# Last down matrices in three column parts, the final norm's vector applied by feature, other matrices loaded early, the expert list made at another place

## The reference: two decoder layers with experts

```
for i in range(DEPTH):                                   # DEPTH = 2
    mod = silu(c) @ ada_w[i] + ada_b[i]
    sh1, sc1, g1, sh2, sc2, g2 = split(mod, 6)
    h = modulate(x, norm_mix_g[i], sh1, sc1)
    m, S = retention_mixer(...) if i == 0 else gla_mixer(...)
    x = x + g1 * m
    h = modulate(x, norm_ffn_g[i], sh2, sc2)
    f = moe_ffn(h, ...)          # router, 64 experts, top 8, shared expert
    x = x + g2 * f
return rmsnorm(x, final_norm_g), new states
# rmsnorm(x, g) = x * rsqrt(mean(x * x) + 1e-6) * g
# an expert: (silu(x @ w_gate) * (x @ w_up)) @ w_down
```

## Time and profile before

| | |
|---|---|
| median of 3 runs | 1586.08 us (1584.92 to 1588.89) |
| the profiled execution | 1585.7 us, its span 1583.9 us |
| granted TensorE clock, mean | 0.989 of full |
| layer 0, experts | about 356 to 889 us |
| layer 1, experts | about 1030 to 1575 us |
| DMA | 580 MB, 366 GB/s over the span |

### The profile page before, as it was taken

The page is one execution under the profiler, slowest core; times in us unless marked ns, Lnnn a source line. Parts: engine busy times, 40 slices in busy tenths (PEclk is TensorE's granted clock), DMA queues, the critical chain, the costliest instruction groups (busy, mean ns, idle before and its releaser), DMA issues. The chain is left out here.

```text
span 1583.9 us, 29421 instructions
## 1 busy us (share of the span) xinstructions
PE 1492.9 (94%) x11132; PEld 983.6 (62%) x11132; DVE 701.7 (44%) x1998; ACT 357.8 (23%) x760; POOL 92.0 (6%) x117
## 2 busy tenths in 40 slices
PE   6999998999999999999996899999999999999976
PEld 4778765687665566566553587777566566565533
DVE  3204534315465535534354335453754544543543
ACT  3012443203212111111120255431111211211111
POOL 0000100001000000010000000001000000010000
PEclk9999999999999999999998999999999999999998
DMA  9997699429999999999999983999999999999996
GB/s 364 389 370 267 251 399 399 177 106 359 382 418 420 421 420 420 420 419 419 415 389 415 355 285 109 352 361 338 415 418 421 420 420 420 421 418 415 392 411 245
DMA packets 153295, 580.27 MB, mean 366 GB/s; under 512 B 16893, under 2 KB 62113, under 8 KB 104938
## 3 DMA queue, kind: packets, MB, share of 16 engines
q1 hardware_dynamic: 137642, 535.74, 85.5%
q0 software_dynamic: 14912, 40.91, 6.7%
q10 hardware_dynamic: 640, 2.26, 0.4%
HBM read 566.12 MB, written 26.90 MB: 374 GB/s over the span
## 5 line engine op out<-in xcount | busy, mean ns | idle before, releaser
L2544 PE MATMUL ps<-ring,scratch 128*64 128x256 f32 x3008 | 330.6, 380 | 1.3 <-DMA ring<-in_moe_w_up 1.2
L2544 PEld LDWEIGHTS ps<-ring,scratch 128*64 128x64 f32 x3008 | 215.5, 137 | 106.6 <-issue 3.0
L2603 PE MATMUL ps<-ring,scratch 128*64 128x512 f32 x816 | 186.8, 598 | 1.2 <-DVE scratch L2961 0.9
L716 PE MATMUL ps<-hT,ring 128*128 128x264 f32 x768 | 182.1, 392 | 1.3 <-ACT hT L401 1.3
L2501 PE MATMUL ps<-scratch 128*128 128x264 bf16 x1344 | 165.8, 276 | 3.7 <-DVE xT L2864 2.0
L716 PEld LDWEIGHTS ps<-hT,ring 128*128 128x128 f32 x768 | 146.8, 193 | 31.6 <-issue 2.8
L2889 DVE SCALAR_TENSOR_TENSOR scratch<-scratch,ps 128x256 f32<-128x256 f32 x60 | 28.8, 480 | 300.3 <-ACT scratch L2998 279.7
L2501 PEld LDWEIGHTS ps<-scratch 128*128 128x128 bf16 x1344 | 116.7, 97 | 53.7 <-issue 15.4
L2856 DVE TENSOR_TENSOR scratch<-scratch,ps 128x264 f32<-128x264 f32 x224 | 95.3, 428 | 65.0 <-PE ps L2501 64.9
L2603 PEld LDWEIGHTS ps<-ring,scratch 128*64 128x64 f32 x816 | 53.3, 136 | 107.0 <-issue 75.1
L2998 ACT ACTIVATE scratch<-ps 128x256 f32<-128x256 f32 x60 | 23.1, 384 | 390.9 <-PE ps L2544 319.6
(11 more groups left out here) (411 smaller groups left out, 1538.5 us busy)
## 6 DMA issues: line engine op xcount, KB each, us to landing
ring<-in_moe_w_up SPq DMA_DIRECT2D x128, 1024.0 KB, 19.0
ring<-in_moe_w_gate SPq DMA_DIRECT2D x124, 1024.0 KB, 18.1
ring<-in_moe_w_down SPq DMA_DIRECT2D x118, 1024.0 KB, 15.5
ring<-in_ada_w SPq DMA_DIRECT2D x48, 1024.0 KB, 12.5
ring<-in_ret_w_in SPq DMA_DIRECT2D x24, 1024.0 KB, 16.8
ring<-in_state_ret SPq DMA_DIRECT2D x16, 1024.0 KB, 14.6
out_ret_sample<-ring POOLq DMA_DIRECT2D x16, 1024.0 KB, 9.0
ring<-in_gla_w_in SPq DMA_DIRECT2D x12, 1024.0 KB, 11.9
```

The costliest lines, as they stand in the source:

```text
L716: mm = nc.tensor.matmul(k.ps[:, bank, 0:T], w[:, c, m * P:(m + 1) * P], k.h[:, c, :], start=(c == 0), stop=(c == DC - 1))
L2544: mm = nc.tensor.matmul(k.ps[lo:lo + CAP, 2 + p, j * DE:(j + 1) * DE], xg[:, p, c, lo:lo + CAP], w[:, c, :], start=(c == 0), stop=(c == DC ...
L2603: mm = nc.tensor.matmul(k.ps[lo:lo + CAP, 6 + half, :], hid_t[:, p, m, lo:lo + CAP], w[:, m, half * 512:(half + 1) * 512], start=(m == 0), ...
```

## The change

Seven edits, in both expert layers where nothing else is said.

1. The early loads are matrices 2 and 3 of round 0 (the up matrices of experts 0 and 1) in place of 0 and 1; SP issues the two of round 1 that take their ring slots before the third down matrix of round 0, no longer behind it. `AHEAD` is the first down matrix.
2. The product that orders the ranks stands behind one chunk of the second shared up product, no longer behind three; `list_order` comes directly behind the sum of the weights.
3. DVE splits the weights (`w_parts`) behind the shared hidden products; PE's `slots_first` stands behind four chunks of the shared down product, no longer two.
4. In the last round the down matrices come in columns 0 to 511, 512 to 767 and 768 to 1023, each with its own semaphore. PE makes the second part behind chunks 0 and 1, the third behind 2 and 3.
5. ACT squares chunks 0 and 1 between the copies of the parts, the others behind the load of the square root's table.
6. Layer 1: DVE multiplies each chunk of `k.x` by the gain vector, one number a feature, before it is transposed; ACT squares the chunk as it is; PE sums the squares with the squares as weights and one column of ones. The load of the spread gain vector goes.
7. At the end DVE scales three of the four half rows, ACT the fourth and the samples; POOL has no part, and the order of SP's stores is another.

```diff
-EARLY = 2
+EARLY = (2, 3)
-    AHEAD = ("moe_w_down", 2)
+    AHEAD = ("moe_w_down", 0)
+    EARLY_LOADS = [ROUND[i] for i in EARLY]
+    gained = acc
+    final_sq = row_area[:, D:3 * D].rearrange("p (c t) -> p c t", c=DC)
...
+    LAST_PARTS = [(0, 512, 6, 0), (512, 768, 7, 0), (768, 1024, 7, 256)]
...
-        load_until(k, sp, n_sh + 3 + RING - 1)
+        load_until(k, sp, n_sh + 3 + RING - 2)
         sp.wait_ge(s_count, 1)
-        for name, e in ROUND[0:EARLY]:
+        for name, e in EARLY_LOADS:
...
+        load_until(k, sp, n_sh + 3 + RING - 1)
         wait_used(k, sp, n_sh + 1)
...
-        for half in range(2):
-            cols = slice(half * 512, (half + 1) * 512)
+        for i, (c0, c1, _, _) in enumerate(LAST_PARTS):
+            cols = slice(c0, c1)
...
+    def last_down(i):
+        c0, c1, bank, at = LAST_PARTS[i]
+        for m in range(FC):
+            for e, lo in LIGHT_BLOCKS:
+                n = place("moe_w_down", e, LIGHT_PLACE)
+                mm = nc.tensor.matmul(k.ps[lo:lo + 32, bank, at:at + c1 - c0], hid_t[:, 0, m, lo:lo + 32],
+                                      slot(k, n, D)[:, m, c0:c1], start=(m == 0), stop=(m == FC - 1))
...
     def last_spread(pe, follow):
...
+        chunk(0)
+        chunk(1)
+        pe.wait_ge(s_third_quarter, 16 * EPI)
+        last_down(1)
+        chunk(2)
+        chunk(3)
+        wait_light(pe, LAST, "moe_w_down")
+        pe.wait_ge(s_part, 2 * d + 2)
+        last_down(2)
+        for c in range(4, DC):
+            if c == 6:
+                pe.wait_ge(s_part, 2 * d + 3)
+            if follow and c == 4:
+                follow(pe, 0)
+                follow(pe, 1)
+            chunk(c)
+            if follow:
+                follow(pe, c - 2)
...
+    def squares_sum(t, c):
+        t0, n = TOKENS[t]
+        nc.tensor.matmul(k.ps[:, 6 + t, 0:1], final_sq[:, c, t0:t0 + n], ones[:, 0:1], start=(c == 0),
+                         stop=(c == DC - 1))
     def x_rows(pe, c):
+        pe.wait_ge(s_gained, c + 1)
+        for t, (t0, n) in enumerate(TOKENS[0:2]):
+            nc.tensor.transpose(k.ps[:, 2 + 2 * t + c // 4, (c % 4) * P:(c % 4 + 1) * P], gained[:, c, t0:t0 + n], ident)
+        pe.wait_ge(s_squares, c + 1)
+        squares_sum(0, c)
+        for b in range(DC // 2 + 1) if c == DC // 2 else range(c, c + 1) if c > DC // 2 else ():
+            squares_sum(1, b)
...
-        shared(1, 1, range(LIST_AT))
+        shared(1, 1, range(1))
         pe.wait_ge(s_ranked, 1)
...
+            if beside and i < BESIDE_COPIES:
+                act.wait_ge(s_add, DC * (LAST + 1) + i + 1)
+                beside(act, i)
...
+        def gain(c):
+            nc.vector.tensor_scalar(gained[:, c, :], k.x[:, c, :], k.fin_g[:, c:c + 1], None, ALU.mult)\
+                .then_inc(s_gained, 1)
...
         if layer:
+            for c in range(DC):
+                nc.tensor.transpose(k.ps[0:NS, c // 4, (c % 4) * P:(c % 4 + 1) * P], gained[:, c, TP:T], ident)
+            pe.wait_ge(s_squares, DC + 1)
+            for c in range(DC):
+                mm = nc.tensor.matmul(k.ps[0:NS, 6, 1:2], small[:, c, :], ones[:, 0:1], start=(c == 0),
+                                      stop=(c == DC - 1))
```

More of the change, by code:

```diff
@@ L317, in load_early @@
 def load_early(k, sp, layer):
-    for i in range(EARLY):
-        n = k.stage[f"moe{layer}"] + i
+    for i, at in enumerate(EARLY):
+        n = k.stage[f"moe{layer}"] + at
         wait_slot(k, sp, n - RING)
@@ L1943, in gla, with rows, store @@
     release_semaphores(k, old)
[L1948 to L1968, removed]
 def final(k, behind):
     nc, out = k.nc, k.out
-    s_ms, s_rt, s_rs, s_half, s_scaled, s_small, s_st = (k.sem(f"y_{n}") for n in (
-        "meansq", "root", "rstd", "half_rows", "samples_scaled", "samples", "stored"))
+    s_ms, s_rt, s_rs, s_half, s_last, s_st = (k.sem(f"y_{n}") for n in (
+        "meansq", "root", "rstd", "half_rows", "last_half_rows", "stored"))
     y = k.scratch[:, 0:TT * D].rearrange("p (t d) -> p t d", t=TT)
-    scaled = k.scratch[:, TT * D:TT * D + D]
     meansq, root, rstd = (k.scratch[:, (TT + 1) * D + 4 * i:(TT + 1) * D + 4 * i + TT] for i in range(3))
-    sums = behind.sums
-    n_gain = k.stage["final_gain"]
-    gain = slot(k, n_gain, D)[:, 0, :]
+    def rows(t, half):
+        return y[:, t, half * 512:(half + 1) * 512], k.ps[:, 2 + 2 * t + half, :], rstd[:, t:t + 1]
+    def store(eng, t, half):
+        eng.dma_start(out["y_prompt"][0, t * P:(t + 1) * P, half * 512:(half + 1) * 512], rows(t, half)[0])\
+            .then_inc(s_st, 16)
     with nc.Block() as block:
@@ L2186, in experts @@
     else:
-        s_final = k.sem(f"{tag}_final_rows_then_small_squares")
+        s_final, s_gained, s_squares = (k.sem(f"{tag}_final_{n}") for n in ("sums", "gained", "squares"))
     h_done = k.sem(f"{tag}_heavy_step")
@@ L2594, in pe_round @@
                 wait_light(pe, r, "moe_w_down")
-            for half in range(1 if last else 2):
+            if last:
+                last_down(0)
+            for half in range(0 if last else 2):
                 four_down(0, LIGHT_BLOCKS, half, LIGHT_PLACE)
@@ L3374, in tail_vector @@
                         .then_inc(x_add, 1)
+            if layer:
+                v.wait_ge(x_add, pairs * DC + DC)
+                for c in range(DC):
+                    gain(c)
             v.br(done)
@@ L3377, in tail_vector @@
         with nc.body(usual, valid_engines=here):
-            finish()
+            finish(gain if layer else None)
             v.br(done)
@@ L3382, in tail_vector, with square @@
             nxt.vector(v)
+    def square(act, c):
+        if layer == 0:
+            nxt.square(act, c)
+        else:
+            nc.scalar.activation(final_sq[:, c, :], k.x[:, c, 0:TP], ACT.Square, scale=D ** -0.5).then_inc(s_squares, 1)
     def tail_scalar(act):
@@ L3424, in tail_scalar @@
         nc.scalar.activation(silu[0:1, 0, 0:1], ident[0:1, 0:1], ACT.Sqrt)
+        for c in range(BESIDE_COPIES, DC):
+            act.wait_ge(s_add, DC * (LAST + 1) + c + 1)
+            square(act, c)
         if layer == 0:
```

158 lines of the change are left out of this document (73 added, 85 removed).

## The result

| | median us | runs | ratio to before (95%) | profiled execution | its span |
|---|---|---|---|---|---|
| before | 1585.95 | 17 | | 1585.70 | 1583.9 |
| after | 1592.09 | 17 | 1.0035 (1.0025 to 1.0045) | 1588.96 | 1587.1 |

The change makes the kernel slower by 5.6 us (4.0 to 7.1, the ratio's 95% interval). The forecast was 1586.4, no change, with a range that ends at 1589.8. It was wrong.

What follows compares the result with a forecast made beforehand. PE, busy 94% of the span, was taken as the bound, with loads only just keeping up. Terms -1.2 - 1.0 + 0.4 + 2.1 = +0.3 us gave 1586.4 us, no change, range 1582.3 to 1589.8.

Steps and rivals of the forecast that it cites:

- Loads of round 1 earlier: Both expert layers: earlier loads give a 1.5 us lead that ends heavy-round waits of 0.88 and 0.33 us: -1.2 us.
- DVE's order: Shared down product: weight splitting moved later ends PE's waits for DVE of 0.39 and 0.58 us: -1.0 us.
- Three parts, layer 0: Layer 0's end: smaller pieces land loads 0.6 us later; the first GLA product waits for its matrix: +0.4 us.
- Layer 1's end: Last down matrices and final norm: reciprocal 3.1 us later, some regained at the stores, so the end moves +2.1 us.
- The walk: Layer 1's end, priced step by step from the last down product through chunks, sums and transposes: reciprocal at 1580.4, was 1577.32.
- Rival C: Layer 1's end: sums at 0.38 us each move the end +3.4; +2.1 in all, 1588.2 us; chance 0.15.
- Rival A: Layer 1's end: cheap sums at 0.05 us each, end only +0.4; -2.4 in all, 1583.7 us; chance 0.20.
- Rival B: Expert rounds: the loads' 3.7 us lead lasts to both layer ends, -7.3 instead of -1.2; 1580.3 us; chance 0.08.

Runs made afterwards that it cites:

- e13: Kernel before with only the other early and ahead matrices and the early loads issued one load sooner, instruction order as before: 1585.88 us, ratio 1.0007.
- e2: Kernel before with only the last down matrices in three column parts, both layers; routing and final norm as before: 1585.47 us, ratio 1.0002.
- e11: Kernel before with only the final norm by feature; last down matrices in halves, routing as before: 1590.97 us, ratio 1.0028.
- e12: Kernel before with only the routing's other instruction order (list earlier, weights later, shared products split elsewhere); early matrices as before: 1583.66 us, ratio 0.9985.
- e1: Kernel before with only the routing's part (early and ahead matrices, instruction order); last down matrices and final norm as before: 1586.37 us, ratio 0.9999.
- e3: Changed kernel with the final norm as before, so routing and three parts only: 1585.79 us, ratio 1.0000.
- e14: Kernel before with the routing's other instruction order and the last down matrices in three parts; early matrices and norm as before: 1584.04 us, ratio 0.9988.
- e4: Changed kernel with the last down matrices in two halves again; routing and final norm by feature as changed: 1591.63 us, ratio 1.0035.
- e8: Changed kernel with ScalarE's table load moved ahead of the last round's copies, both layers, nothing left out: 1591.03 us, ratio 1.0027.
- e5: Changed kernel with fourteen of the sixteen one-column sums of squares left out: 1588.44 us, ratio 1.0010.
- e6: Changed kernel without the eight multiplications by the final norm's gain vector: 16.88 us to the reciprocal, one execution.
- e7: Changed kernel with six of the samples' eight transposes at the very end left out: 17.76 us to the reciprocal, one execution.
- e10: Changed kernel with squares added on GpSimd (two sums left on PE), samples' transposes beside each chunk, table load early: 1589.17 us, ratio 1.0011.

## Why the prediction was wrong

*Loads of round 1 earlier, lead of 1.5 us, -1.2.* **This step failed.** The loads went out where it said (389.4 and 405.0 on the clock of before), and still the waits in the heavy rounds did not end: 2.4 us in after, 2.3 in e13 with the loads alone, whose ratio is 1.0007. The lead of a few loads was no more there ten rounds on. And the 1.2 us were read from one execution, as if they belonged to the kernel: e2 and e11, with the same routing, wait 2.5 and 2.4 us.

*DVE's order, -1.0.* Right in mechanism: both waits at the shared down product are gone, the first stages are 0.6 and 0.8 us shorter, 1.4 in all, and e12 alone is faster by 2.4 us (1.0 to 4.0). Together with the loads no gain was measured (e1, 0.9999); the traces have the heavy rounds 1.1 us a layer longer there than before. The prediction let the two steps add up. Why they don't isn't shown, and in whole times the intervals of e1 and e12 overlap.

*Three parts, layer 0, +0.4.* Right, by three executions. The engines gain (e2, 0.8 us to the conditioning product), but the first GLA product waits for its matrix in e2, e3 and e14 and starts 19.66, 20.06 and 20.11 us after the down product instead of 19.54: +0.1 to +0.6. In e2 the window in which the quarters' 1 KB pieces come (872 to 876 us) moved 349 GB/s, as the prediction had taken from the earlier trace rows. In after, PE was itself late by the low clock and found its matrix there.

*Layer 1's end, +2.1.* **This is the term that was mis-sized most: it measures +4.1.** To the reciprocal it is 18.84 - 14.37 = +4.5; from there to the end 6.30 us against 6.56 to 6.79 in the kernels with the norm by row, -0.4. The walk itself was good: a sum 0.23 us (six in 1.40, predicted 1.38), chunk 4 to chunk 7 5.11 us (predicted 4.95), chunk 7 to the reciprocal 5.04 in e4 and e8 (predicted 4.9). Three things were missing:
- 1.05 us of low clock. The granted clock was 1.00 up to 1577.5, then 0.50 (the level of 1.2 GHz), and the samples' transposes took 1.87 us. In six executions that have all eight of them at the end they took 1.03 us four times (e4, e5, e6, e8) and 1.87 twice (after, e11); e7, with two of them, had the low clock too. The walk priced them at full clock, and which of the two comes isn't told by the program: e4's ends with the same instructions as e11's (18.61 us against 19.79).
- 0.65 us at the stores. The end was to get 1.0 us back and got 0.3 to 0.5. The profile doesn't show when these stores land. But the samples' store went out 1.9 us sooner after the reciprocal than in e1 (issued by +2.5 us against +4.4), SP's last one 0.5 us sooner (+2.8 against +3.3), and the end came 0.3 us sooner. That fits an end that goes with SP's store; no run tests it. The prediction had let it go with both.
- 0.35 us of the walk itself. Counted from the down product (1561.46, less the 1.3 us by which it was cold), it came to the reciprocal after 17.45 us; at full clock it is 17.8 (18.84 - 1.05).

So the sum by what was measured is 0 (routing, e1, to 2 us either way) + 4.1 (layer 1's end, parts included; 3.1 where the clock stays full) + 0.1 to 0.6 (layer 0's end): 3.2 to 4.7, against 5.6 (4.0 to 7.1) for the whole. For the norm alone it is +4.4 (2.7 to 6.3), and the traces have 3.9 (by e4) to 5.0 (by e11). So the loss is the norm's, to within the intervals; whether 1 us more lies elsewhere stays open.

*Rival C* (slower, by the sums) had the right place and the right sign, at +3.4 for the end; its price a sum (0.38) was wrong, so part of that agreement is luck: the clock and the stores filled the gap. Its chance of 0.15 was too low, because the forecast counted 2.2 us of gains as safe. Rival A (cheap sums) falls by the 0.23 us. Rival B (the lead is kept) falls by the waits. *The clock and the pages:* by the row a sum was to take 0.28, by the page 0.21; the trace says 0.23, nearer the page's estimate (the Trainium skill, "TensorE: Matmul & The Clock Gate", "LDWEIGHTS (loading the stationary operand)"). The forecast had taken 0.23, so the price of a sum was not what failed.

## What to carry to other kernels

A sum over partitions with one moving column took PE 0.23 us where it had 128 columns of weights and 0.07 where it had 8. Sixteen of them stood between products that a chain over three engines waited for, and fourteen, with the wait for a square among them, cost 3.2 us. The row sums on ScalarE of before were the cheaper way here (13.9 us to the reciprocal with parts); adding up on GpSimd first and leaving two sums came to 15.65. A gain that is read from waits in one execution is no safe term of a sum: the same routing showed 1.2, 2.4 and 2.5 us of such waits. And a path at the end of a program is best measured from its last common event over several executions: here that repeats to 0.03 us (low clock apart) where whole executions scatter by 7.

## What the runs showed of the hardware

- GpSimd's 128x256 f32 additions (0.72 us) held up VectorE's 128x8 additions, until they ended themselves: 0.16 us became 0.35 to 0.62, and a gain of 0.35 became 0.82 (from 1579.10, with additions at 1579.04 to 1579.76 and from 1579.91). The step that reads the accumulation memory was not held up (e10).
- The load of ScalarE's table (1.28 us) cost 1.0 us at the chunks where it stood before squares that PE waited for, and nothing in ScalarE's wait of 4 us ahead of the last round's copies (e8).
- The same program text reached the first router product at 366.0 to 372.0 us in the sixteen profiled executions, before any changed instruction.
- The scatter of whole executions goes with the granted clock. Over 117 executions of before the time falls as the mean clock rises (correlation -0.74): a median of 1590.5 us in the six at 0.984, 1582.0 in the five at 0.990.
- One-column products of 128 weight columns come at the pace of their weight loads: twelve loads 1.42 us, twelve products 1.40 (after).
